# Norms behind output projections in halves of the tokens, and another opening, in a three-layer fp32 model

## The reference

```python
# layer 1                                  # layers 2 and 3, l = 0, 1
x = x + 0.5 * swiglu(rms_norm(x, ffn1_norm), ffn1_w_in, ffn1_w_out)
x = x + mix @ w_mix_out                    # h = h + g1 * (attention_output @ wo)
x = x + 0.5 * swiglu(rms_norm(x, ffn2_norm), ffn2_w_in, ffn2_w_out)
                                           # hn = rms_norm_2(h, norm2_g[l]) * (1 + sc2) + sh2
                                           # h = h + g2 * conv_ffn(hn, win, conv_w, conv_b, wout)
def rms_norm(x, g):
    return x * lax.rsqrt(jnp.mean(x * x, axis=-1, keepdims=True) + EPS) * g
```

## Time and profile before

| | us |
|---|---|
| median of 3 runs (2302.18 to 2304.47) | 2302.79 |
| the profiled execution | 2299.5 |
| its span | 2298.0 |
| PE busy | 2223.4 |
| DVE busy | 1270.5 |
| ACT busy | 950.2 |
| POOL busy | 268.2 |

### The profile page before, as it was taken

How to read it: one execution, slowest core, us unless ns; L and a number is a source line. 1 busy time by engine, 2 the same in 40 slices (tenths; PEclk the granted TensorE clock), 3 DMA queues, 4 the chain that set the end, 5 groups by cost and what they waited for, 6 DMA issues and landing times.

```text
span 2298.0 us, 31235 instructions
## 1 busy us (share of the span) xinstructions
PE 2223.4 (97%) x11568; PEld 1831.8 (80%) x11568; DVE 1270.5 (55%) x2069; ACT 950.2 (41%) x1460; POOL 268.2 (12%) x442
## 2 busy tenths in 40 slices
PE   7999999998999999999999999999989999999998
PEld 6788887977778888887878788888878887888886
DVE  5754764456743363355356656456466655654654
ACT  4222223347644323324246554254253645533542
POOL 2110220035400020010036000000000430000000
PEclk9999999998999999999999999999999999999999
DMA  7864983231033283273321233333212012323332
GB/s 245 275 210 122 317 289 96 92 103 38 11 117 102 87 281 108 79 256 118 96 76 59 73 91 96 106 84 89 86 63 82 30 38 74 91 92 100 91 96 87
DMA packets 258720, 266.92 MB, mean 116 GB/s; under 512 B 8854, under 2 KB 201917, under 8 KB 258637
## 3 DMA queue, kind: packets, MB, share of 16 engines
q1 hardware_dynamic: 236909, 187.20, 27.2%
q0 software_dynamic: 21728, 78.63, 9.9%
HBM read 263.62 MB, written 12.66 MB: 120 GB/s over the span
## 4 chain that ended last, share of the span: by engine, by line
PE 86%; DVE 6%; ACT 4%; DMA 1%; POOL 1%; issue 1%; DVEq 0%; SPq 0%; POOLq 0%; ACTq 0%
PE bank L340 15%; PE bank L341 15%; PE bank L342 15%; PE bank L346 11%; PE bank L348 11%; PE bank L347 11%; PE bank L1567 2%; PE bank L1518 2%; PE bank L1542 2%; DVE w_lo L323 1%; ACT probs L1603 1%; POOL probs L1725 1%; DMA mod_w_more<-in_mod_w_dram 1%; PE bank L667 1%; DVE xT_lo L642 1%
## 5 line engine op out<-in xcount | busy, mean ns | idle before, releaser
L323 DVE TENSOR_TENSOR w_lo<-raw,w_hi 128x2048 fp32r<-128x2048 f32 (+3 forms) x202 | 415.6, 2057 | 374.2 <-ACT w_hi L319 371.5
L340 PE MATMUL bank<-xT_hi,w_hi 128*128 128x512 f32 x1560 | 609.6, 391 | 6.1 <-DVE xT_lo L642 4.2
L342 PE MATMUL bank<-xT_hi,w_lo 128*128 128x512 f32 x1560 | 607.8, 390 | 0.0
L341 PE MATMUL bank<-xT_lo,w_hi 128*128 128x512 f32 x1560 | 607.8, 390 | 0.0
L319 ACT ACTIVATE w_hi<-raw 128x2048 fp32r<-128x2048 f32 (+3 forms) x202 | 348.4, 1725 | 484.0 <-PE bank L348 429.9
L340 PEld LDWEIGHTS bank<-xT_hi,w_hi 128*128 128x128 f32 x1560 | 292.5, 188 | 73.3 <-DVE xT_lo L642 8.8
L342 PEld LDWEIGHTS bank<-xT_hi,w_lo 128*128 128x128 f32 x1560 | 292.5, 188 | 62.3
L341 PEld LDWEIGHTS bank<-xT_lo,w_hi 128*128 128x128 f32 x1560 | 292.4, 187 | 60.0
L346 PE MATMUL bank<-w_hi,hid_hi 128*128 128x512 f32 x704 | 277.8, 395 | 0.0
L347 PE MATMUL bank<-w_lo,hid_hi 128*128 128x512 f32 x704 | 277.8, 395 | 0.0
L348 PE MATMUL bank<-w_hi,hid_lo 128*128 128x512 f32 x704 | 277.7, 395 | 0.0
(11 more groups left out here) (303 smaller groups left out, 2858.8 us busy)
## 6 DMA issues: line engine op xcount, KB each, us to landing
raw<-in_ffn_w_in_dram SPq DMA_DIRECT2D x40, 1024.0 KB, 6.1
raw<-in_f_win_dram SPq DMA_DIRECT2D x40, 1024.0 KB, 6.0
mod_w<-in_mod_w_dram POOLq DMA_DIRECT2D x48, 512.0 KB, 5.3
mod_w_more<-in_mod_w_dram POOLq DMA_DIRECT2D x48, 512.0 KB, 5.6
raw<-in_ffn_w_out_dram SPq DMA_DIRECT2D x24, 768.0 KB, 4.5
raw<-in_f_wout_dram SPq DMA_DIRECT2D x24, 768.0 KB, 4.4
raw<-in_a_wqkv_dram SPq DMA_DIRECT2D x12, 1024.0 KB, 5.1
skewed_strips<-bias_strips POOLq DMA_DIRECT2D x32, 320.0 KB, 6.4
```

Source lines behind the costliest of these rows:

```text
L323: dve.tensor_tensor(out=w_lo[:, slot, :n], in0=raw[:, slot, :n], in1=w_hi[:, slot, :n].bitcast(f32), op=ALU.subtract).then_inc(lo_done, 1)
L340: pe.matmul(o, lhsT=w[0], rhs=xs[0], start=first, stop=False)
L341: pe.matmul(o, lhsT=w[0], rhs=xs[1], start=False, stop=False)
L342: return pe.matmul(o, lhsT=w[1], rhs=xs[0], start=False, stop=last)
```

## The change

Norms behind the three output projections become `HalfNorm`, in two halves of 256 tokens:
- PE runs panel 1 as A on blocks 0 and 1, B on 0 and 1, A on 2 and 3, then transposes blocks 0 and 1 (half 0), then B on 2 and 3. The Ffn's first pair is done as 96 matmuls of 256 columns: half 0 for both banks, the transposes of blocks 2 and 3, half 1.
- ACT and DVE write `xT_hi` and `xT_lo` of half 0 in two groups of four tiles, between them the statistics and additions of blocks 2 and 3. Blocks 0 and 1 are scaled by DVE, blocks 2 and 3 by ACT (`scale_act`). In modulated norms the shifted tiles go to `act_g` (four places) instead of `full` (two).
- The split of B stays on ACT behind `row_and_rope`, and the modulated gain is computed before it on DVE.

The opening: each block of x has its own semaphore; the first weight pair u = 1 is loaded before the constants; ACT begins with a small Sqrt (`root_table`); ACT waits for the gain only before it writes `xT_hi`; eight matmuls of 128 columns that nobody reads stand before the transposes of the last tile (`BUSY`); the constants' transposes come after the first pair, into banks 4 and 5; DVE copies them in the first pair's work and makes the strips during the first output chunks. On PE, and in the first Ffn on DVE, the loop over the two halves is written out.

```diff
         class Norm:
...
+                    if self.n == 0 and t == KT - 1:
+                        for _ in range(BUSY):
+                            pe.matmul(self.banks[t][:, 0:P], lhsT=ident[:, :], rhs=ident[:, :], start=True, stop=True)
...
+        class HalfNorm(Norm):
...
+            def scale_act(self, act, s):
+                act.wait_ge(n_rs, self.root_n + s + 1)
+                act.activation(self.tile(s), x[:, s, :], ACT.Copy, scale=small[:, 8 + s:9 + s]).then_inc(n_xn, 1)
...
+            def half_pe(self, pe, h):
+                for s in (2 * h, 2 * h + 1):
+                    pe.wait_ge(n_xn, self.n + s + 1)
+                    for t in (0, 2, 1, 3, 4, 6, 5, 7):
+                        ins = pe.transpose(self.place(h, t)[:, s % 2 * P:(s % 2 + 1) * P], self.tile(s)[:, t * P:(t + 1) * P],
+                                           ident[:, :])
+                        if s % 2 and t // 2 % 2:
+                            ins.then_inc(n_T, 1)
...
+            def half_act(self, act, h, ts):
+                for t in ts:
+                    hi = xT_hi[:, t, PAIR * h:PAIR * (h + 1)]
...
+                        if t // 2 % 2:
+                            self.lo_ready(act, h, t - 2)
+                        act.activation(hi, self.place(h, t), ACT.Identity, scale=self.gains[:, t:t + 1],
+                                       bias=zero[:, :]).then_inc(n_hi, 1)
...
         class Ffn:
...
+                def by_halves():
+
+                    pe.wait_ge(lo_done, self.pair_c(0, 0, 0) + 1)
+                    pe.wait_ge(pair_free[0], EVEN * 2 * self.n + 1)
+                    for part in range(2):
+                        if part:
+                            self.norm.half_pe(pe, 1)
+                        for kt in range(KT):
+                            self.norm.lo_ready(pe, part, kt)
+                            for b, done in enumerate((g_done, used)):
+                                last = feature_major(pe, bank[b][:, PAIR * part:PAIR * (part + 1)],
+                                                     w_part(self.slot(0), (b * KT + kt) * P, P),
+                                                     xT_part(kt, PAIR * part, PAIR), kt == 0, kt == KT - 1)
...
         class MixOut:
...
-                self.gemm.pe(pe, 1)
...
+                self.gemm.piece(pe, 1, 0, [0, 1])
+                self.gemm.piece(pe, 1, 1, [0, 1])
+                self.gemm.piece(pe, 1, 0, [2, 3])
+                norm.half_pe(pe, 0)
+                self.gemm.piece(pe, 1, 1, [2, 3])
...
+            def act(self, act, norm, between=None, gained=None):
+                self.gemm.split_act(act, 0)
+                if between:
+                    between(act)
+                c = self.gemm.panels[1][3]
+                next_hi(act, c)
+                for s in range(2):
+                    norm.stats_act(act, s)
+                next_hi(act, c + 1)
+                if gained is not None:
+                    act.wait_ge(*gained)
+                norm.half_act(act, 0, range(4))
+                norm.stats_act(act, 2)
+                norm.half_act(act, 0, range(4, KT))
+                norm.stats_act(act, 3)
+                for s in range(2, TOK):
+                    norm.scale_act(act, s)
+                norm.half_act(act, 1, range(KT))
...
+                c = self.gemm.panels[1][3]
+                next_lo(dve, c)
+                for s in range(2):
+                    add(1, s)
+                for s in range(2):
+                    norm.scale_dve(dve, s)
+                next_lo(dve, c + 1)
+                norm.half_dve(dve, 0, range(4))
+                for s in range(2, TOK):
+                    add(1, s)
+                norm.half_dve(dve, 0, range(4, KT))
+                for s in range(2, TOK):
+                    norm.inverse_dve(dve, s)
+                norm.half_dve(dve, 1, range(KT))
...
-        norm_ffn1 = Norm(lambda s: [(x_in, 64), (cols_done, 1)], column("ffn1_norm", KT))
+        norm_ffn1 = Norm(lambda s: [(x_in[s], 16)], column("ffn1_norm", KT))
...
-            ffn1.pair_sp(sp, 0, 0, 0)
+            for u in range(2):
+                ffn1.pair_sp(sp, 0, 0, u)
             constants_load(sp)
...
+            root_table(act)
+            norm_ffn1.act(act, (cols_done, 1), lambda act: split_hi(act, 2, 0, landed(2)))
...
-            norm_ffn1.part(pe, 3)
-            constants_pe(pe)
-            ffn1.pe(pe)
+            ffn1.pe(pe, constants_pe)
```

More of the change, by code:

```diff
@@ L746, in half @@
                 def half(h, done=0):
-                    for u in range(done, 2 if done else 0):
-                        self.pair_sp(sp, h, 0, u)
                     with sp.Fori(1 if done else 0, PAIRS2) as i:
@@ L765, in sp, with pe @@
                         half(h)
-            def pe(self, pe):
+            def pe(self, pe, between=None):
                 def tile(o, slot, lo, first=False):
                     for kt in range(KT):
-                        if first:
+                        if first and self.norm.parts == 1:
                             self.norm.part(pe, kt)
@@ new lines, in by_halves @@
+                def by_halves():
[10 more added lines that the diff above has]
+                                                     xT_part(kt, PAIR * part, PAIR), kt == 0, kt == KT - 1)
+                                if part and kt == KT - 1:
+                                    last.then_inc(done, 1)
@@ new lines, in half @@
+                def half(h, first=False):
+                    if first:
+                        if self.norm.parts == 2:
+                            by_halves()
+                        else:
+                            pair(h, 0, 0)
+                        if between:
+                            between(pe)
+                        pair(h, 0, 1)
+                    with pe.Fori(1 if first else 0, PAIRS2) as i:
+                        for u in range(2):
+                            pair(h, i, u)
@@ L914, in one, with half @@
                             mod_columns(dve, k)
-                with dve.Fori(0, 2) as h:
-                    with dve.Fori(0, PAIRS2 - 1) as i:
+                def half(h, first=None, later=None):
+                    if first:
+                        one(h, 0, 0, first)
+                        one(h, 0, 1)
+                    with dve.Fori(1 if first else 0, PAIRS2 - 1) as i:
                         for u in range(2):
@@ L970, in dve @@
                         add(TOK - 1)
+                if first:
+                    half(0, first, later)
+                    half(1)
+                else:
+                    with dve.Fori(0, 2) as h:
+                        half(h)
         class TokenGemm:
@@ new lines, in dve @@
+                for s in range(TOK):
+                    add(0, s)
+                if between:
+                    between(dve)
+                if modulate:
+                    modulate(dve)
+                c = self.gemm.panels[1][3]
[6 more added lines that the diff above has]
+                norm.half_dve(dve, 0, range(4))
@@ L2682, in _ @@
             out_1.dve(dve, norm_ffn2)
-            norm_ffn2.dve(dve, TOK - 1)
             ffn2.dve(dve)
```

187 lines of the change are left out of this document (112 added, 75 removed).

## The result

The changed kernel takes 2307.62 us (median of 20 runs, 2304.03 to 2315.09); the kernel before took 2301.10 in as many runs beside it (2295.52 to 2304.47). The ratio is 1.0035, 95% interval 1.0028 to 1.0043: slower by 0.35%. The profiled spans differ by about as much, 2305.7 against 2298.0, and split at the places of the prediction they show where the 7.7 us came from in this pair of executions (a second pair, under before_again and after_again, differs by 13.0). A0 is the first matmul of a projection's panel 1, the event the first matmul of the Ffn's second pair.

What follows compares the result with a forecast made beforehand. TensorE, busy 2223.4 of 2298.0 us, was taken as the bound. Opening -6.1, the three projections +2.0, +5.6 and +0.5, clock +1.7 and +3.4 sum to +7.1: 2302.8 becomes 2309.9 us, range 2299 to 2315.

Steps and rivals of the forecast that it cites:

- the likeliest case: Whole kernel: the forecast itself, slower by 4.6 to 10 us, chance 0.50.
- Opening: Start to the Ffn's second weight pair: reached at 30.7 us against 36.82, 6.1 saved, between 3.5 and 7.3.
- lands at 13.1 and caps the gain: Opening: the first weights' load lands at 13.1 us, so w_hi moves from 15.78 to 13.1, 2.7 earlier.
- B: Second weight chunk of panel 1: in the second projection its split follows the rope's tables, so PE stands still 5.1 us.
- Its clock: Second projection: the 5.1 us wait for B drops the granted clock to its lower level, costing 1.7 us.
- D: Weights of the Ffn's second pair, split behind the whole norm: PE waits 2.8 to 3.8 us in all three places.
- to be had at most: Projection's end to the event: gain limit, 2.2 us in the first place, 6.8 in the second and third.
- D is not late: Rival, Ffn's second pair: D's w_lo is done before part 1 ends; -6.5 us in all, 2296.3; chance 0.10.
- Clock behind D: After the three waits for D: two of three halve the clock, 3.4 us, bounds 0 to 5.1.
- Scaling by ScalarE: Norms behind the projections: had DVE kept the scaling, 0.6 us would be saved in each.
- 256 columns: Ffn's first pair: 96 matmuls of 256 columns take 11.5 us for 10.9, 0.6 more for each norm.
- The strips and the unrolled loop: Strips cost nothing in the first output chunks, where DVE is mostly idle; PE's unrolled loop nothing, between -1 and +1.

Runs made afterwards that it cites:

- before_again: The kernel before, unchanged, profiled a second time and not timed against it; its first attention took 28.84 us.
- after_again: The changed kernel, unchanged, profiled a second time and not timed beside the kernel before; second projection 52.20 us, third 44.22, A0 to event.
- b_first: Changed kernel with the split of B put ahead of the rope's tables on both engines; 2302.3 us, ratio 1.0013 to the kernel before.
- fill_waits: Changed kernel with filler transposes where PE waits: 40 ahead of B in the second projection, 24 ahead of D in all three; 2303.2 us, ratio 1.0020.
- no_fillers: Changed kernel without the eight filler matmuls of the opening; 2313.37 us, ratio 1.0063 to the kernel before.
- d_early: Changed kernel with the split of D moved ahead of the norm's second half in all three places; 2296.7 us, ratio 0.9991 to the kernel before.
- best: Changed kernel with B ahead of the rope's tables, DVE scaling the last two blocks, D's w_hi behind the last statistics, w_lo behind half 1; 2286.8 us, ratio 0.9946.
- scale_dve: Changed kernel with the last two token blocks scaled by VectorE again, as in the kernel before; 2306.3 us, ratio 1.0034.
- second_load_back: Changed kernel with the load of the second pair's weights back behind the constants' loads; 2310.77 us, ratio 1.0055 to the kernel before.
- opening_only: The kernel before with the new opening alone, output projections and their norms as before; 2291.84 us, ratio 0.9973.
- both: Changed kernel with B ahead of the rope's tables and D ahead of the norm's second half; 2289.0 us, ratio 0.9957 to the kernel before.

## Why the prediction was right, step by step

**In sum** +7.1 was forecast, +7.7 in the spans and +6.5 in the medians were measured, 2309.9 against 2307.6. It lies in the likeliest case and by its own mechanism. That the sums agree this closely is partly luck. They hide errors of both signs (opening 1.0 short, 2.5 won where 0 was forecast, second projection 1.4 longer), and the second pair of profiles differs by 13.0. The +6.5 depends on how many runs fell in each kernel's upper group of times, 10 of 20 before and 5 of 20 after; group against group the change costs 8.7 and 11.2 (last section). And 1.7 of the 2.3 between 2309.9 and 2307.6 is the median before, 2302.8 in three runs and 2301.1 in twenty.

**Opening: -6.1 forecast, -5.07 up to the event.** ACT's start at 5.1 came true (5.09), and so did the fillers (2.42 for them, the first matmul 18.9 forecast, 19.87 measured), the clock and the constants' 0.87. The step that failed is "lands at 13.1 and caps the gain": I took the landing time of before for one that the change leaves alone, and it lands 1.7 later. The fillers hid most of it, since PE's own transposes ended at 19.3 anyway, at half clock down to 16.4.
I had stopped counting at the event. Behind it another 2.53 were won in this pair of profiles: the split of the following weights used to be late (PE waited 1.16 at 59.90 and 0.29 at 103.96; now 0.29 and nothing), and in the profile of before the norm ahead of the mix projection ran into half clock (5.62 from its transposes to the first matmul, 4.74 after). The second is a draw of the clock (4.74 in before_again). The first is not shown to be the change's: the two waits sum to 1.45 and 0.91 in the two profiles of before and to 0.29 and 0.84 in the two of the changed kernel. For it speaks that the nine other profiles with the new opening have no such wait there at all.

**B: 5.1 forecast, 4.80 measured**, by the step forecast; b_first shows that the split's place behind the rope's tables is the whole cause. **Its clock: 1.7 forecast, 2.6 to 2.85 measured** (fill_waits, b_first). The mis-sized term is the length at half clock: I took 3.4 us from the stretches of before, here the granted clock was 0.52 over the 6 us behind the wait, which is 5.8 at half clock. It isn't the same each time: over the 6 us behind the same wait no_fillers has

```profile
1285.30:1291.30 6.00, 6.00 (x19) 0.72 0.63 175
```

which is 3.4 at half clock, and its second projection is 1.0 shorter. The 1.7 was the right price for a short fall.

**D: 2.8 to 3.8 forecast, 2.95, 3.59 and 3.59 measured.** The hand-made queue for the third place gave ACT's first tile of half 1 33.45 behind A0, its last end 38.35, the event 43.85; the trace has 33.08, 38.52 and 44.21. That was the expensive part of the working, and it paid: it is what told a loss from the 6.8 "to be had at most". d_early confirms the cause. The rival "D is not late" is what best turns the kernel into.

**Clock behind D: two falls of three, 3.4, forecast.** The profile has two (first and third), and 0.58 + 0.89 + 1.67 = 3.1 in the stretches behind the events, not all of it the clock's. That two of three came true is luck. The other five profiles with these waits unfilled (after_again, b_first, scale_dve, no_fillers, second_load_back) have three falls each, so 17 of 18 waits of 2.95 to 3.60 brought one, and what such an execution pays behind D is nearer the 5.7 of after_again than 3.4. The one wait without a fall is 3.59 long, and 2.95 brought one: why that one was spared stays open.

**Scaling by ScalarE: 0.6 in each forecast; 0.33, 0.79 and 0.90 measured.** **256 columns: 0.6 more in each forecast.** The second half's 48 matmuls took 673.82 to 679.67, 0.122 each for 0.120.

**The strips and the unrolled loop at nothing** agree with opening_only, whose gain of 6.2 to 7.2 (by ratio and by median) is the 6.7 expected without a cost of theirs; one of 1 us could hide in its interval.

## What to carry to other kernels

When a piece of work is cut in halves so that PE can start early, everything that was hidden behind the uncut piece is asked for sooner: list each weight chunk needed within the next pieces, and where its split stands in the queues of both engines that make it. Write those queues out by hand with durations of the trace; here this gave four waits to within 0.3 us. Then put each split into a gap in which its engine waits for PE anyway (w_hi of D behind the last statistics), not merely earlier: the same split one step sooner gave back up to 2.2 of the 2.95 that it saved. And price a fall of the clock from several profiles, not from one.

## What the hardware showed beyond that

**One kernel's times fall in two groups, 4.5 to 8 us apart.** The 20 runs of the changed kernel are 15 between 2304.0 and 2308.7 and 5 between 2312.4 and 2315.1; those of before split as 10 and 10 around 2298.6 and 2303.1; fill_waits has six of 2298.7 to 2300.2 and six of 2306.2 to 2308.1. The profiles show a place: the first attention, from a named wait for probs to the matmul behind a named wait for q_lo, takes 28.4 to 28.9 us in eight of thirteen profiles and 33.7 to 33.8 in five (b_first, both, no_fillers, fill_waits, best), also where the code up to there is the changed kernel's, as in b_first. The rows of b_first, and the windows of TensorE over the stretch in the changed kernel and then in b_first:

```profile
497.51 2.44 PE L1677 MATMUL bank<-ident,probs 128*128 128x128 f32 x6 [1.50 <-DVE probs L1860]
...
531.34 1.55 PE L1702 MATMUL bank<-score,v_tok 128*64 128x128 f32 x12 [1.98 <-DVE q_lo L1779]
```

```profile
490.00:560.00 70.00, 60.95 (x537) 0.83 0.27 84
```

```profile
490.00:560.00 70.00, 60.30 (x471) 0.76 0.25 76
```

The longer form has more of half clock, and in the same five profiles the norm ahead of the mix projection, 100 us earlier, already takes 5.8 to 6.2 from its transposes to the first matmul, 4.74 in the others but before (5.62). That these two forms are the two groups of times is likely, not shown. For it: each of the five profiled executions with the long form is in the upper half of its kernel's times, 2307.99 in b_first where the other ten are 2300.8 to 2304.3, and those of the changed kernel, d_early, scale_dve, opening_only and second_load_back, with the short form, are in the lower half. A median of few runs may sit in either group or between them, which is why 5 us of a median weigh less here than 1 us of a place. Group against group (medians of each) the changed kernel is 8.7 and 11.2 slower than before, where the medians of all runs differ by 6.5.

**A half clock's stretch isn't of one length.** Behind B it was 6.8 us long in the changed kernel and 3.4 in no_fillers, behind D 3.4 or 6.8, and the same wait of 3.59 in the second place went with 0 (changed kernel), 3.4 (after_again) or 6.8 (scale_dve) of it.
